# The last expert's w_down taken by column halves, with the next block's first slot and half of its first projection in between

## The chip, the cores and the metric

The kernel runs on one NeuronCore of a Trainium2 chip. The metric is the device time of one execution in microseconds (us). The engines are TensorE (PE; its weight loads are PEld), VectorE (DVE), ScalarE (ACT), GpSimd (POOL) and SyncE (SP), which issues nearly all transfers.

## The reference

Two blocks in float32 on 256 tokens of width 1024. The first is a mixing layer followed by a mixture of experts with expert choice; the second begins with a norm and the projections of two attentions.

```python
# first block, second half: 16 experts, each takes 32 tokens
xe = h2[idx]                                   # (16, 32, 1024)
a  = einsum('becd,edf->becf', xe, w_gate_e)    # 1024 x 2048 per expert
u  = einsum('becd,edf->becf', xe, w_up_e)
y  = einsum('becf,efd->becd', silu(a) * u, w_down_e)   # 2048 x 1024 per expert
x  = x + gate_f * scatter_add(y * vals, idx)
x  = rms_norm(x, g_final)
# second block
h  = rms_norm_2(x, mix_norm_g)
u  = h @ w_in                                  # q_diff = the first 512 of its columns
...
```

## The kernel before, in words

**Slots.** All weights pass through a ring of 16 places in SBUF, each 128 partitions x 2048 floats (1 MB, one *slot*). Slots are numbered through the whole kernel: the head, 16 experts of 24 slots (8 of gate, 8 of up, 8 of down), then the tail (`FIRST_TAIL` on). SP issues the loads in this order; each waits until the slot whose place it takes has been used. The count of used slots is the semaphore `slot_used`, which TensorE raises.

**One expert (`expert`, TensorE, line 1133 on).** The 32 tokens are the stationary operand, 128 rows by 32 columns, so four products can stand beside each other in four column groups of the array (`tile_position`), writing four partition groups of a PSUM bank. Gate and up: per slot four products, one in each group (line 1142). The hidden values are turned (line 1157) and kept as `act_t`. Down (line 1169): a slot holds 2 rows of the contraction per partition and all 1024 output columns; its four products go to 2 groups and 2 banks (bank 2 and bank 3, for the column halves n = 0 and 1). When all 8 slots are through, VectorE evicts bank 2 and bank 3 into `y` (line 2081), and TensorE scatters `y` back to token order with 128 x 256 products into banks 4 to 7, which hold the residual stream transposed: two products for each quarter q of the columns (line 1180). The last 8 down slots of the last expert are loaded one by one, each with 8 KB in one piece per partition.

**Second block's entry.** ScalarE and VectorE split the stream's quarters into a high and a low float32r part (`split_stream`: `ht_hi` on ScalarE, line 1385; `ht_lo` on VectorE, line 1773), and likewise each weight slot (`split_entry` for the halves of the first slot, lines 1400 and 1788; `split_ahead` for whole slots, lines 1380 and 1763). A projection of rows (`rows_product`) multiplies three combinations of the parts (lines 734 to 736): `q_diff` has 48 such products, in 4 pairs of k. Pair by pair it waits for the parts; after the third pair `turn_stream_back` (line 1207) turns the stream into rows again, which needs ScalarE's copies `xt` of all four quarters (`stream_kept`, line 1641). Then come `k_diff` and the rest of `TAIL_UNITS`. The two slots of `q_diff` are loaded after all down slots (lines 660 and 662); POOL loads the attention bias when the first of them has been used (line 716).

**The order around the change** is written out by hand, engine by engine; no planner is involved. `keep_busy(n)` (line 903) issues n products of constants into a bank whose content nobody needs; the kernel before uses it only at the start.

Of the kernel before, what the change touches and what calls it, by code (L numbers as in the profile page):

```python
# [24 lines left out]
P = 128  # L25
# [91 lines left out]
def build(nc, t, out):  # L117
    ctx = ExitStack()
    with ctx:
# [432 lines left out]
        def _(sp):  # L552
# [94 lines left out]
            for e, n in loads_between((NE - 2) * EXPERT_SLOTS, NE * EXPERT_SLOTS - 4):  # L647
                sp.wait_ge(slot_used, HEAD_SLOTS + released(e + n - 1))
                load_expert(NE // 2 - 1, e, n)
            for e in range(NE * EXPERT_SLOTS - 4, NE * EXPERT_SLOTS):  # L650
                sp.wait_ge(slot_used, HEAD_SLOTS + released(e))
                load_expert(NE // 2 - 1, e, 1)
            for n, src in enumerate(tail_stream):
                s = FIRST_TAIL + n

                sp.wait_ge(slot_used, FIRST_TAIL - TAIL_RING + n + 1 if n < TAIL_RING else s - TAIL_RING + 1)
                if s == first_slot["q_diff"]:
                    for half, name in enumerate(OPENING[0:2]):
                        rows = slice(2 * half, 2 * half + 2)
                        sp.dma_start(slot_in(s, k=FG, n=BANK)[:, rows, :], src[:, rows, :]).then_inc(opening_loaded[name], 16)  # L660
                else:
                    sp.dma_start(slot_in(s, k=src.shape[1], n=src.shape[2]), src).then_inc(loaded[place(s)], 16)
# [57 lines left out]
        def _(pe):  # L720
            mm = nc.tensor.matmul

            def end_first(ins):
                ins.then_inc(first_ready, 1)
# [13 lines left out]
            def split_slot(s, **dims):  # L738

                if s == first_slot["q_diff"]:  # L740
                    pe.wait_ge(first_lo, STEPS * len(OPENING) + 1)
                else:
                    pe.wait_ge(lo_ready, len([n for n in split_no if n <= s]))
                return [shaped(ring_r[p][:], **dims) for p in (part_place[s], place(s))]
# [88 lines left out]
            def rows_product(s, u, await_pair=None):  # L833

                for i in range(2):
                    w = split_slot(s + i, k=FG, n=BANK)
                    for pair in range(2) if await_pair else (None,):
                        if await_pair:
                            await_pair(2 * i + pair)
                        for tt in range(TT):  # L840
                            for kk in (2 * pair, 2 * pair + 1) if await_pair else range(FG):
                                k = FG * i + kk
                                last = split_product(bank(2 * (u % 2) + tt), [a[:, k, tt * P:(tt + 1) * P] for a in (ht_hi, ht_lo)],
                                                     [h[:, kk, :] for h in w], k == 0, k == KD - 1)
                            if k == KD - 1 and tt == 0:
                                end_first(last)
                        if await_pair and i and pair == 0:
                            turn_stream_back()
                    last.then_inc(slot_used, 1)

# [52 lines left out]
            def keep_busy(n):  # L903

                for _ in range(n):
                    mm(psum[:, 2, 0:P], ones, ones, start=True, stop=True)
# [218 lines left out]

            def expert(i, h, looped=False, side=False):
# [34 lines left out]
                pe.wait_ge(cur_ready, 2 * i + (h + 2))  # L1161

# [12 lines left out]
                for n in range(2):  # L1175
                    pe.wait_ge(y_ready, 4 * i + (2 * h + n + 1))
                    for q in (2 * n, 2 * n + 1):
                        for c in range(2):
                            at = (2 * q + c) * P - n * BANK
                            last = mm(bank(4 + q, c=2, s=SEQ)[:, c, :], y[:, n, at:at + P], gwt.rearrange("p t m -> p (t m)"),  # L1180
                                      start=False, stop=True, skip_group_check=True)
                        last.then_inc(scattered, 1)
# [10 lines left out]

            def await_entry(pair):

                pe.wait_ge(norm_lo, pair + 1)
                if pair == 1:
                    pe.wait_ge(lo_ready, split_no[first_slot["q_diff"]] + 1)
# [41 lines left out]
            for u, (name, slots) in enumerate(TAIL_UNITS):  # L1240
# [6 lines left out]
                elif name in ("z0", "z1"):  # L1247
                    transposed_product(first_slot[name], u, (ht_hi, ht_lo))
                elif name in IN2_CHUNK:
                    rows_product(first_slot[name], u, await_entry if u == 0 else None)  # L1250
# [83 lines left out]
        def _(act):  # L1334
# [58 lines left out]
            def split_entry(half):  # L1393

                s = first_slot["q_diff"]
                cols = slice(half * SLOT // 2, (half + 1) * SLOT // 2)
                act.wait_ge(opening_loaded[OPENING[half]], 16 * (STEPS + 1))
# [325 lines left out]
        def _(dve):  # L1723
# [45 lines left out]
            def split_pair(q, b, scale, at):  # L1769

                dve.wait_ge(norm_hi, at + q + 1)
                for k in (2 * q, 2 * q + 1):
                    ins = V.scalar_tensor_tensor(ht_lo[:, k, :], bank(b, c=2, s=SEQ)[:, k % 2, :], scale[:, k:k + 1],
                                                 ht_hi[:, k, :].bitcast(F32), ALU.mult, ALU.subtract)
                ins.then_inc(norm_lo, 1)

            def split_stream(q):
                split_pair(q, STREAM_BANKS[q], mix_gain, 0)

            def split_entry(half):  # L1780

                s = first_slot["q_diff"]
# [3 lines left out]
                else:  # L1786
                    dve.wait_ge(first_hi, STEPS * len(OPENING) + 1)
# [283 lines left out]
            def expert(i, h):  # L2071
# [6 lines left out]
                V.tensor_tensor(act_h, bank(1), sig_a, ALU.mult).then_inc(act_ready, 1)  # L2078
                dve.wait_ge(slot_used, 2 * EXPERT_SLOTS * i + (HEAD_SLOTS + (h + 1) * EXPERT_SLOTS))
# [9 lines left out]
            expert(NE // 2 - 1, 1)  # L2089
# [298 lines left out]
```

## Time and profile before

| | |
|---|---|
| runs of the kernel before | 1314.24 us median of 3 (1312.12 to 1315.41) |
| profiled execution | 1314.88 us, span 1313.1 us |
| mean granted TensorE clock | 0.875 of full |
| TensorE busy | 979.5 us (75%) |
| VectorE / ScalarE busy | 378.1 / 247.5 us |
| HBM read | 494.71 MB, 378 GB/s over the span |

All times in the rows count from the start of the span. The granted clock is TensorE's, as a share of 2.4 GHz: 0.50 is 1.2 GHz. A busy time of TensorE counts the modelled ends of pipelined products, so start-to-start distances tell more than the duration of one.

### The profile page before, as it was taken

What the parts mean: (1) busy time and instruction counts of PE and PEld (TensorE: products, weight loads), DVE (VectorE), ACT (ScalarE), POOL (GpSimd) and SP (SyncE); (2) the same over time, 40 slices, a digit from 0 to 9 for tenths busy, and PEclk for the clock granted to TensorE, in tenths of its full rate; (3) what the DMA queues carried; (4) which work ended last, traced back from release to release, by engine and by line L of the source; (5) the groups of instructions that cost most, each with busy time, mean ns of one, the idle gap of its engine ahead of it and who ended that gap; (6) DMA issues with size and microseconds to landing.
All of it is one profiled execution on the core that took longest, in us unless ns stands there. A gap on an engine that the chain in (4) does not pass through costs nothing.

```text
span 1313.1 us, 15613 instructions
## 1 busy us (share of the span) xinstructions
PE 979.5 (75%) x6766; PEld 559.6 (43%) x6766; DVE 378.1 (29%) x575; ACT 247.5 (19%) x375; POOL 21.6 (2%) x47
## 2 busy tenths in 40 slices
PE   8999999878665665655656655657556666899998
PEld 7999998323121221212121221212121221478988
DVE  4698866210000110000010100000010100388865
ACT  4453434001000000000000000000000000467744
POOL 2000200000000000000000000000000000000000
PEclk8999999988787888689798878888786887999999
DMA  9998999899999999999999999999999999965230
GB/s 336 389 377 311 321 389 414 351 430 430 427 434 428 431 431 431 426 434 433 431 431 431 426 431 437 431 430 431 429 427 436 429 430 421 392 234 161 97 128 33
DMA packets 70156, 496.43 MB, mean 378 GB/s; under 512 B 4794, under 2 KB 26954, under 8 KB 49632
## 3 DMA queue, kind: packets, MB, share of 16 engines
q1 hardware_dynamic: 67792, 489.11, 90.4%
q0 software_dynamic: 2080, 6.55, 1.5%
q8 instruction: 35, 0.57, 0.2%
q10 hardware_dynamic: 240, 0.11, 0.0%
q14 instruction: 9, 0.07, 0.0%
HBM read 494.71 MB, written 1.06 MB: 378 GB/s over the span
## 4 chain that ended last, share of the span: by engine, by line
DMA 56%; PE 42%; DVE 1%; issue 1%; ACT 0%; ACTq 0%; SPq 0%; DVEq 0%
DMA ring<-in_w_down_e 23%; DMA ring<-in_w_up_e 18%; DMA ring<-in_w_gate_e 15%; PE psum L734 8%; PE psum L735 8%; PE psum L736 8%; PE psum L1142 7%; PE psum L1169 4%; PE psum L1180 1%; PE psum L885 1%; PE psum L1222 1%; PE psum L1077 0%; DMA arena<-in_b_ada 0%; PE psum L797 0%; PE psum L1257 0%
## 5 line engine op out<-in xcount | busy, mean ns | idle before, releaser
L1142 PE MATMUL psum<-ring,arena 128*32 128x512 f32 x2048 | 304.2, 743 | 192.8 <-DMA ring<-in_w_up_e 111.6
L1169 PE MATMUL psum<-ring,arena 128*32 128x512 f32 x976 | 162.2, 800 | 98.1 <-DMA ring<-in_w_down_e 97.5
L1142 PEld LDWEIGHTS psum<-ring,arena 128*32 128x32 f32 x2048 | 70.8, 130 | 385.8 <-issue 179.0
L1169 PEld LDWEIGHTS psum<-ring,arena 128*32 128x32 f32 x976 | 42.8, 137 | 203.9 <-issue 143.7
L1763 DVE TENSOR_TENSOR ring_r<-ring,ring_r 128x2048 fp32r<-128x2048 f32 x49 | 111.1, 2289 | 36.6 <-ACT ring_r L1380 36.4
L1540 ACT ACTIVATE arena<-psum 128x512 f32<-128x512 f32 x16 | 9.6, 598 | 535.2 <-PE psum L1142 535.2
L734 PE MATMUL psum<-ht_hi,ring_r 128*128 128x256 f32 x384 | 109.5, 285 | 0.0
L735 PE MATMUL psum<-ht_lo,ring_r 128*128 128x256 f32 x384 | 108.1, 281 | 0.0
L736 PE MATMUL psum<-ht_hi,ring_r 128*128 128x256 f32 x384 | 107.6, 280 | 0.0
L2081 DVE TENSOR_TENSOR arena<-psum,arena 128x512 f32<-128x512 f32 x32 | 20.6, 686 | 290.0 <-PE psum L1169 290.0
L1380 ACT ACTIVATE ring_r<-ring 128x2048 fp32r<-128x2048 f32 x49 | 92.4, 1910 | 29.2 <-PE psum L736 24.1
L2074 DVE TENSOR_TENSOR arena<-psum,arena 128x512 f32<-128x512 f32 x16 | 11.1, 692 | 270.9 <-ACT arena L1540 270.9
L734 PE MATMUL psum<-ring_r,ht_hi 128*128 128x256 f32 (+1 forms) x256 | 87.0, 340 | 0.2 <-issue 0.2
L736 PE MATMUL psum<-ring_r,ht_lo 128*128 128x256 f32 (+1 forms) x256 | 86.9, 339 | 0.0
L735 PE MATMUL psum<-ring_r,ht_hi 128*128 128x256 f32 (+1 forms) x256 | 86.1, 336 | 0.0
L734 PEld LDWEIGHTS psum<-ht_hi,ring_r 128*128 128x128 f32 x384 | 72.1, 188 | 1.9 <-issue 1.5
L736 PEld LDWEIGHTS psum<-ht_hi,ring_r 128*128 128x128 f32 x384 | 72.5, 189 | 0.0
L735 PEld LDWEIGHTS psum<-ht_lo,ring_r 128*128 128x128 f32 x384 | 72.4, 189 | 0.2
L1180 PE MATMUL psum<-arena 128*128 128x256 f32 x256 | 61.4, 394 | 13.6 <-DVE arena L2081 13.6
L1544 ACT ACTIVATE arena<-psum 128x512 f32<-128x512 f32 x16 | 9.6, 597 | 297.5 <-PE psum L1157 297.5
L1180 PEld LDWEIGHTS psum<-arena 128*128 128x128 f32 x256 | 48.6, 195 | 36.4 <-DVE arena L2081 30.1
L734 PEld LDWEIGHTS psum<-ring_r,ht_hi 128*128 128x128 f32 x256 | 48.1, 188 | 6.4 <-issue 1.1
(291 smaller groups left out, 921.8 us busy)
## 6 DMA issues: line engine op xcount, KB each, us to landing
ring<-in_w_gate_e SPq DMA_DIRECT2D x23, 4096.0 KB, 33.4
ring<-in_w_up_e SPq DMA_DIRECT2D x22, 4096.0 KB, 33.0
ring<-in_w_down_e SPq DMA_DIRECT2D x21, 4096.0 KB, 33.8
ring<-in_w_up_e SPq DMA_DIRECT2D x16, 2048.0 KB, 36.5
ring<-in_w_in SPq DMA_DIRECT2D x31, 1024.0 KB, 9.7
ring<-in_w_gate_e SPq DMA_DIRECT2D x14, 2048.0 KB, 36.2
ring<-in_w_down_e SPq DMA_DIRECT2D x14, 2048.0 KB, 36.9
ring<-in_w_ada SPq DMA_DIRECT2D x16, 1024.0 KB, 10.3
```

The costliest lines, as they stand in the source:

```text
L734: mm(to, left[0], right[0], start=start, stop=False)
L735: mm(to, left[0], right[1], start=False, stop=False)
L736: return mm(to, left[1], right[0], start=False, stop=stop)
L885: last = mm(psum[32 * g:32 * g + 32, 6, st % 2 * P:(st % 2 + 1) * P], c_rep[:, k, :], w[:, kk, g * P:(g + 1) * P], start=(k == 0), stop=(k ...
L1142: last = mm(psum[32 * g:32 * g + 32, b, :].rearrange("s (q c) -> s q c", c=4), cur[h][:, k, :], w[:, g // 2, :, g % 2 * 4:g % 2 * 4 + 4], ...
L1169: last = mm(psum[32 * q:32 * q + 32, 2 + n, :], act_t[:, f % 4, (f // 4) * CAP:(f // 4 + 1) * CAP], w[:, kk, n * BANK:(n + 1) * BANK], sta ...
L1180: last = mm(bank(4 + q, c=2, s=SEQ)[:, c, :], y[:, n, at:at + P], gwt.rearrange("p t m -> p (t m)"), start=False, stop=True, skip_group_ch ...
L1222: last = mm(bank(4 + 2 * m + c, j=2, s=SEQ)[:, j, :], q[r, 2 * m + j, (a % 2) * P:(a % 2 + 1) * P], k[r, 2 * m + j, :], start=True, stop=T ...
L1380: f(ring_r[part_place[s]][:], ring[:, place(s), :], ACT.Copy).then_inc(hi_ready, 1)
L1763: V.tensor_tensor(ring_r[place(s)][:], ring[:, place(s), :], ring_r[part_place[s]][:].bitcast(F32), ALU.subtract).then_inc(lo_ready, 1)
L2074: V.tensor_tensor(sig_a, bank(0), sig_a, ALU.mult).then_inc(gated, 1)
L2081: V.tensor_tensor(y[:, n, :], bank(2 + n), gf_row[:, n * BANK:(n + 1) * BANK], ALU.mult).then_inc(y_ready, 1)
```

## The change

The eight last down slots of the last expert (called D0 to D7 here) are loaded by column halves: D0 to D3 hold all 2048 rows of the contraction for columns 0 to 511, D4 to D7 for columns 512 to 1023. In a slot each partition has 4 rows, each a piece of 2 KB, and its four products go to the four column groups of the array. The first slot of `q_diff` is loaded between D3 and D4, into the place of another slot that comes free sooner. `q_diff`'s second slot now comes in halves too.

TensorE's order at the end of the last expert was: 8 down slots, 4 quarters of scatter, `q_diff` pairs 0, 1, 2, turn of the stream, pair 3. It becomes: D0, 4 constants, D1, 4 constants, D2, 4 constants, D3, 2 constants; scatter of quarters 0 and 1; `q_diff` pair 0; D4, D5; pair 1; D6, D7; scatter of quarter 2 and 3; pair 2 (column by column of k), turn of the stream, pair 3. VectorE evicts the first half of `y` after D3 and the second half in two steps of 256 columns after D7. ScalarE and VectorE split the entry slots' halves and the quarters in the new order. The first entry slot counts as used together with D7, and the bias's load waits for that count.

```diff
@@ place
-            return TAIL_START + (s - FIRST_TAIL) % TAIL_RING
+            return tail_room[0] if s == FIRST_TAIL else TAIL_START + (s - FIRST_TAIL) % TAIL_RING
@@ sync
-            for e in range(NE * EXPERT_SLOTS - 4, NE * EXPERT_SLOTS):
-                sp.wait_ge(slot_used, HEAD_SLOTS + released(e))
-                load_expert(NE // 2 - 1, e, 1)
+            def load_last_down(j):
+                n, block, part = j // 4, j % 4 // 2, j % 2
+                rows = t["w_down_e"][0][NE - 1].rearrange("(b p k) n -> b p k n", b=2, k=KD)[block]
+                at = expert_place(last_down + j)
+                sp.wait_ge(slot_used, HEAD_SLOTS + released(last_down + j))
+                sp.dma_start(shaped(ring[:, at, :], k=4, n=BANK), rows[:, 4 * part:4 * part + 4, n * BANK:(n + 1) * BANK]).then_inc(loaded[at], 16)
+            def load_entry(i):
+                s = FIRST_TAIL + i
+                for half in range(2):
+                    rows = slice(2 * half, 2 * half + 2)
+                    done = loaded[place(s)] if i and half else opening_loaded[OPENING[2 * i + half]]
+                    sp.dma_start(slot_in(s, k=FG, n=BANK)[:, rows, :], tail_stream[i][:, rows, :]).then_inc(done, 16)
+            for j in range(4):
+                load_last_down(j)
+            sp.wait_ge(slot_used, FIRST_TAIL - RING + 1)
+            load_entry(0)
+            for j in range(4, 8):
+                load_last_down(j)
...
@@ tensor
+            def entry_pair(pair):
+                s = first_slot["q_diff"] + pair // 2
+                by_column = pair == 2
+                pe.wait_ge(*((part_lo, KD + 1) if by_column else (norm_lo, pair + 1)))
+                if pair % 2:
+                    pe.wait_ge(lo_ready, split_no[s] + 1)
+                else:
+                    pe.wait_ge(first_lo, STEPS * len(OPENING) + 1 + pair // 2)
...
+            def scatter(q):
+                for c in range(2):
+                    k = 2 * q + c
+                    last = mm(bank(4 + q, c=2, s=SEQ)[:, c, :], y[:, k // 4, k % 4 * P:(k % 4 + 1) * P], gwt.rearrange("p t m -> p (t m)"),
+                              start=False, stop=True, skip_group_check=True)
+                last.then_inc(scattered, 1)
+            def last_down(j):
+                n, at = j // 4, expert_place(NE * EXPERT_SLOTS - 8 + j)
+                arrived(pe, FIRST_TAIL - 8 + j)
+                w = shaped(ring[:, at, :], k=4, n=BANK)
+                for kk in range(4):
+                    f = 4 * (j % 4) + kk
+                    last = mm(psum[32 * kk:32 * kk + 32, 2 + n, :], act_t[:, kk, (f // 4) * CAP:(f // 4 + 1) * CAP], w[:, kk, :],
+                              start=(f < 4), stop=(f >= 12), tile_position=(0, 32 * kk))
+                return last
...
+            for j in range(4):
+                last_down(j).then_inc(slot_used, 1)
+                keep_busy(4 if j < 3 else 2, 3)
+            pe.wait_ge(y_ready, 2 * NE - 1)
+            scatter(0)
+            scatter(1)
+            entry_pair(0)
+            last_down(4).then_inc(slot_used, 1)
+            last_down(5).then_inc(slot_used, 1)
+            entry_pair(1)
+            last_down(6).then_inc(slot_used, 1)
+            last_down(7).then_inc(slot_used, 2)
+            for half in range(2):
+                pe.wait_ge(y_ready, 2 * NE + half)
+                scatter(2 + half)
...
+                elif name == "q_diff":
+                    entry_pair(2)
+                    turn_stream_back()
+                    entry_pair(3).then_inc(slot_used, 1)
@@ scalar
-            split_entry(0)
+            split_entry(0, 0)
             split_stream(0)
-            split_entry(1)
+            split_entry(0, 1)
             split_stream(1)
+            split_entry(1, 0)
             split_stream(2)
-            split("q_diff", 1)
             split_stream(3)
+            split_entry(1, 1)
@@ vector
-            split_entry(0)
+            dve.wait_ge(slot_used, FIRST_TAIL - 4)
+            V.tensor_tensor(y[:, 0, :], bank(2), gf_row[:, 0:BANK], ALU.mult).then_inc(y_ready, 1)
+            split_entry(0, 0)
             split_stream(0)
-            split_entry(1)
+            split_entry(0, 1)
             split_stream(1)
-            dve.wait_ge(scattered, 4 * NE)
+            dve.wait_ge(slot_used, FIRST_TAIL)
+            for half in range(2):
+                cols = slice(half * HALF, (half + 1) * HALF)
+                V.tensor_tensor(y[:, 1, cols], bank(3)[:, cols], gf_row[:, BANK + half * HALF:BANK + (half + 1) * HALF], ALU.mult).then_inc(y_ready, 1)
+            split_entry(1, 0)
             split_stream(2)
-            split("q_diff", 1)
             split_stream(3)
+            split_entry(1, 1)
```

## Rows read from the trace of the kernel before

**Rows 1.** The page's chain that ended last, by engine and by line.
```profile
DMA 56%; PE 42%; DVE 1%; issue 1%; ACT 0%; ACTq 0%; SPq 0%; DVEq 0%
...
DMA ring<-in_w_down_e 23%; DMA ring<-in_w_up_e 18%; DMA ring<-in_w_gate_e 15%; PE psum L734 8%; PE psum L735 8%; PE psum L736 8%; PE psum L1142 7%; PE psum L1169 4%; PE psum L1180 1%; PE psum L885 1%; PE psum L1222 1%; PE psum L1077 0%; DMA arena<-in_b_ada 0%; PE psum L797 0%; PE psum L1257 0%
```

**Rows 2.** Stretches of the span: length, busy time by engine, granted clock, DMA, GB/s.
```profile
1150.00:1313.10 163.10, 156.69 (x996) 137.68 (x994) 122.63 (x171) 101.38 (x172) 0.00 (x0) 1.00 0.39 129
1110.00:1116.50 6.50, 4.77 (x20) 1.32 (x20) 0.69 (x1) 0.23 (x1) 0.00 (x0) 0.50 1.01 422
1118.00:1120.00 2.00, 2.00 (x14) 0.40 (x6) 0.00 (x0) 0.37 (x2) 0.00 (x0) 0.50 0.98 410
1120.00:1122.50 2.50, 2.49 (x20) 0.51 (x14) 0.00 (x0) 0.00 (x0) 0.00 (x0) 0.99 1.01 423
1127.00:1137.00 10.00, 7.97 (x37) 4.03 (x34) 4.00 (x6) 3.57 (x7) 0.00 (x0) 1.00 1.04 387
1122.50:1130.60 8.10, 5.73 (x24) 1.13 (x24) 0.00 (x0) 0.00 (x0) 0.00 (x0) 1.00 1.02 405
```

**Rows 3.** TensorE in order of time: start, length, idle before and its releaser.
```profile
1100.85 3.64 PE L1142 MATMUL psum<-ring,arena 128*32 128x512 f32 x32 [2.31 <-DMA ring<-in_w_up_e]
...
1110.65 3.64 PE L1142 MATMUL psum<-ring,arena 128*32 128x512 f32 x16 [2.98 <-DMA ring<-in_w_up_e]
...
1116.92 5.57 PE L1169 MATMUL psum<-ring,arena 128*32 128x512 f32 x32 [0.69 <-ACT arena L1544]
```

**Rows 4.** The chain that ended last, in order of time, from 1099 us.
```profile
1099.05 31.52 DMA ring<-in_w_down_e
1130.61 1.94 PE psum L1169 x8
1132.57 0.70 DVE arena L2081
1133.32 3.72 PE psum L1180 x16
...
1145.35 1.75 PE psum L1207 x16
...
1149.87 0.23 PE psum L734
```

**Rows 5.** VectorE in order of time: a quarter's low parts, a slot's low part.
```profile
1135.36 0.88 DVE L1773 SCALAR_TENSOR_TENSOR ht_lo<-psum,arena,ht_hi 128x256 fp32r<-128x256 f32 x2 [0.37 <-ACT ht_hi L1385]
...
1145.12 2.29 DVE L1763 TENSOR_TENSOR ring_r<-ring,ring_r 128x2048 fp32r<-128x2048 f32 x1 [2.47 <-ACT ring_r L1380]
```

**Rows 6.** ScalarE: a quarter's high parts, half a slot, three stream copies, the fourth, a slot.
```profile
1134.49 0.84 ACT L1385 ACTIVATE ht_hi<-psum,arena 128x256 fp32r<-128x256 f32 x2 [1.47 <-PE psum L1180]
1135.21 1.05 ACT L1400 ACTIVATE ring_r<-ring 128x1024 fp32r<-128x1024 f32 x1
...
1140.11 1.62 ACT L1641 ACTIVATE arena<-psum 128x512 f32<-128x512 f32 x3
1142.68 0.60 ACT L1641 ACTIVATE arena<-psum 128x512 f32<-128x512 f32 x1 [0.96 <-DVE ht_lo L1773]
1143.17 1.91 ACT L1380 ACTIVATE ring_r<-ring 128x2048 fp32r<-128x2048 f32 x1
```

**Rows 7.** TensorE in the first stage: constants; wide products with narrow ones behind.
```profile
8.61 2.93 PE L906 MATMUL psum<-arena 128*128 128x128 f32 x12
...
24.55 0.28 PE L735 MATMUL psum<-ht_lo,ring_r 128*128 128x256 f32 x1
24.67 0.28 PE L736 MATMUL psum<-ht_hi,ring_r 128*128 128x256 f32 x1
24.88 1.96 PE L885 MATMUL psum<-ring,arena 128*32 128x128 f32 x64
```

**Rows 8.** POOL's issue of the bias, and its size and time to landing.
```profile
1142.88 0.70 POOL L716 DMA_DIRECT2D ring<-in_bias  x1 [881.81 <-PE psum L736]
...
ring<-in_bias POOLq DMA_DIRECT2D x1, 3072.0 KB, 13.6
```

More of the change, by code:

```diff
@@ L738, in split_slot @@
             def split_slot(s, **dims):
[L740 to L743, printed above, removed]
+                pe.wait_ge(lo_ready, len([n for n in split_no if n <= s]))
                 return [shaped(ring_r[p][:], **dims) for p in (part_place[s], place(s))]
@@ L831, in columns_rows, with rows_product @@
                 last.then_inc(slot_used, 1)
-            def rows_product(s, u, await_pair=None):
+            def rows_product(s, u):
                 for i in range(2):
                     w = split_slot(s + i, k=FG, n=BANK)
[L837 to L848, printed above, removed]
-                    last.then_inc(slot_used, 1)
+                    for tt in range(TT):
+                        for kk in range(FG):
+                            k = FG * i + kk
+                            last = split_product(bank(2 * (u % 2) + tt), [a[:, k, tt * P:(tt + 1) * P] for a in (ht_hi, ht_lo)],
+                                                 [h[:, kk, :] for h in w], k == 0, k == KD - 1)
+                        if k == KD - 1 and tt == 0:
+                            end_first(last)
+                    last.then_inc(slot_used, 1)
@@ new lines, in entry_pair @@
+            def entry_pair(pair):
[6 more added lines that the diff above has]
+                    pe.wait_ge(first_lo, STEPS * len(OPENING) + 1 + pair // 2)
+                w = [shaped(ring_r[p][:], k=FG, n=BANK) for p in (part_place[s], place(s))]
+                ks = (2 * pair, 2 * pair + 1)
+                for k, tt in [(k, tt) for k in ks for tt in range(TT)] if by_column else [(k, tt) for tt in range(TT) for k in ks]:
+                    if by_column and (k, tt) == (ks[1], 0):
+                        pe.wait_ge(norm_lo, pair + 1)
+                    last = split_product(bank(tt), [a[:, k, tt * P:(tt + 1) * P] for a in (ht_hi, ht_lo)],
+                                         [h[:, k % FG, :] for h in w], k == 0, k == KD - 1)
+                    if k == KD - 1 and tt == 0:
+                        end_first(last)
+                return last
@@ L1161, in expert @@
                 pe.wait_ge(cur_ready, 2 * i + (h + 2))
+                if not looped and i == NE // 2 - 1 and h == 1:
+                    return
                 for j in range(8):
@@ L1177, in expert @@
                     for q in (2 * n, 2 * n + 1):
[L1178 to L1182, printed above, removed]
+                        scatter(q)
                 if side:
@@ L1391, in split_stream, with split_entry @@
                 split_pair(q, STREAM_BANKS[q], mix_gain)
-            def split_entry(half):
-                s = first_slot["q_diff"]
+            def split_entry(i, half):
+                s = first_slot["q_diff"] + i
                 cols = slice(half * SLOT // 2, (half + 1) * SLOT // 2)
-                act.wait_ge(opening_loaded[OPENING[half]], 16 * (STEPS + 1))
+                if i and half:
+                    arrived(act, s)
+                else:
+                    act.wait_ge(opening_loaded[OPENING[2 * i + half]], 16 * (STEPS + 1))
                 if half == 0:
@@ L1774, in split_pair, with split_entry @@
                                                  ht_hi[:, k, :].bitcast(F32), ALU.mult, ALU.subtract)
+                    if by_column and k % 2 == 0:
+                        ins.then_inc(part_lo, 1)
                 ins.then_inc(norm_lo, 1)
             def split_stream(q):
-                split_pair(q, STREAM_BANKS[q], mix_gain, 0)
-            def split_entry(half):
-                s = first_slot["q_diff"]
+                split_pair(q, STREAM_BANKS[q], mix_gain, 0, by_column=q == 2)
+            def split_entry(i, half):
+                s = first_slot["q_diff"] + i
                 cols = slice(half * SLOT // 2, (half + 1) * SLOT // 2)
@@ L2068, in _, with expert @@
             take(1, 0)
-            def expert(i, h):
+            def expert(i, h, last=False):
                 dve.wait_ge(sig_ready, 2 * i + (h + 1))
@@ L2078, in expert @@
                 V.tensor_tensor(act_h, bank(1), sig_a, ALU.mult).then_inc(act_ready, 1)
+                if last:
+                    return
                 dve.wait_ge(slot_used, 2 * EXPERT_SLOTS * i + (HEAD_SLOTS + (h + 1) * EXPERT_SLOTS))
@@ L2088, in _ @@
             take(NE - 1, NE - 1)
-            expert(NE // 2 - 1, 1)
+            expert(NE // 2 - 1, 1, last=True)
             def split(name, i=0):
```

26 lines of the change are left out of this document (12 added, 14 removed).

## The prediction, made before the changed kernel had run

> **What bounds the kernel now.** I read the chain of work that ended last first [rows 1]: it consists of transfers (56%) and TensorE (42%), and the transfers are the three expert matrices. So the span has a part in which TensorE waits for weights and a part that is TensorE's own. The stage table [rows 2] shows where they meet: DMA moves 405 to 423 GB/s while TensorE is 71% busy between 1122.5 and 1130.6 us (5.73 of 8.10); from 1150 us to the end DMA moves 129 GB/s and TensorE is busy 156.69 of 163.10 us. The chain in order of time [rows 4] gives the seam: the last down slot is issued at 1099.05 and lands at 1130.6; its products take 1.94, the first eviction to `y` 0.70, the scatter 3.72, and then the second block's first projection, `q_diff`, runs. Three quarters of it (36 products from 1137.04 to 1145.35, 0.231 each), the turning back of the stream (1.75 from 1145.35) and its last quarter end where `k_diff` begins: 1149.87 us. After that nothing of the change is left on TensorE, so **the sum is the new time of this one event**.
>
> **The change, part by part.** I lay out the new order on TensorE from 1116.92 us, where the down products begin in both kernels [rows 3]; what comes before is the same.
>
> *Transfers.* A slot is 1.049 MB. Large contiguous pieces come at 423 GB/s, the strided 2 KB rows of `w_in` at 387 [rows 2], so 2.48 and 2.71 us each. The eight last down slots become 2 KB rows, and one entry slot goes ahead of the last four. The first of the eight starts to flow at about 1130.6 - 8 x 2.5 = 1110.6. New landings, one each 2.71: D0 to D3 at 1113.3, 1116.0, 1118.7, 1121.4; entry slot 0 at 1124.1; D4 to D7 at 1126.9, 1129.6, 1132.3, 1135.0. The last lands 4.4 later than now. SP gets one more wait ahead of D4 to D7 (first up slot used, about 1101.8, against 1099.05 for the last issue now [rows 3, 4]): behind it stand four loads with over 20 us to go until they are due, so it costs nothing. POOL's only queued load, the bias, waits for a count that now comes with D7, some 4 us sooner than 1142.88 [rows 8].
>
> *Down products.* Four products of one slot now go to four different column groups. Such slots took 3.64 / 4 = 0.91 us each at full clock and 3.64 / 2 = 1.82 at half (x32 is four slots, x16 two [rows 3]; their clock stands in [rows 2]); the present order takes 1.94 for a lone slot [rows 4].
>
> *Constant products.* Four of them are eight records of 128 columns. The turns of that width took 1.75 / 16 = 0.109 each at full clock [rows 4], so 0.87 for four; the opening's twelve records took 2.93, 0.24 each, 1.95 for four [rows 7]. I take 0.87 at full clock and twice that at half; the other end adds 0.1 to 1 us each.
>
> *Changes between the narrow and the wide array.* In the first stage wide products start 0.12 apart (24.55, 24.67) and the narrow one that follows starts 0.21 later (24.88) [rows 7]: 0.09 us per change. There are 11 where there was one: 1.0 us in all, 0.9 more than now. The lower end is zero, the upper 0.2 each; each is taken as 0.09 below. The Trainium skill's TensorEngine Tiling (Array Packing), section Key Properties, says that changing the tiling mode drains the array. The trace agrees in kind, with these 0.09 us.
>
> *The schedule.* The clock is 0.50 at 1116.92 and rises at 1120.0 [rows 2], under unbroken work, which there is again. D0 to 1118.74; constants, half of them slow, to 1120.29; D1 to 1121.29; constants 1122.25; D2 1123.25; constants 1124.21; D3 1125.21. All four slots landed by 1121.4, so the constants fill no gap here and stand on the path: 2.6 us of the first phase. `y`'s first half 0.70 (two constants hidden beside it), starts of 0.05 at both ends: scatter 0 and 1 run 1126.0 to 1127.86 (eight records at 3.72 / 16). ScalarE starts 0.24 behind scatter 0 as it does now (1133.32 + 0.93, 1134.49 [rows 4, 6]), 0.84 for the high part, VectorE 0.88 for the low [rows 5]: 1128.95, a wait of 1.1 for TensorE. The first pair is 12 products of 0.231: 1131.72. D4 and D5 1133.63, second pair 1136.49, D6 and D7 1138.40. **D7 landed at 1135.0 and TensorE gets to it at 1137.5: the transfers, 4.4 later, are hidden with 2.5 to spare**. Then the new serial tail: 256 columns of `y` 0.44 (by the 0.44 of one column of the low parts), scatter 2 to 1139.85, ScalarE 1140.1 to 1140.95, VectorE's single column to 1141.4, third pair to 1144.2. The stream may be turned back only when ScalarE has copied it: high part of quarter 3 to 1141.9, the last entry half 1.05, four copies of 1.62 / 3 [rows 6] to 1145.1. So TensorE waits 0.9 there, which now is covered (the copies end at 1143.3, the turn begins 1145.35). Turn to 1146.9, last pair to 1149.65.
>
> `k_diff` needs its first slot in both parts: ScalarE 1.91 from 1145.1, VectorE 2.29 [rows 5, 6]: 1149.4, just in time. Its slots land by 1140.5 and 1143.2, before the bias, which needs 13.6 from its issue [rows 8], takes much of the rate.
>
> *Sum.* 1149.65 against 1149.87: 0.2 us sooner. What is gained (24 projection products, 5.5; half the scatter, 1.9; narrower evictions and products, about 1.3) goes back into order: the old seam waited for the last slot at 1130.6; the new one starts its serial tail at 1138.4. The profiled execution took 1314.88, span 1313.1; so 1314.7 for such an execution, and against the median of the runs, 1314.24, **1314.0 us**.
>
> **Rivals.**
> *A, the engine keeps up.* If the clock is already high when D0 starts, 1.5 us go (0.9 of D0, 0.6 of the constants), and if the array changes cost nothing, 1.0 more: 1147.15 at the seam, 2.5 sooner than forecast, 1311.5. It cannot go much further, since TensorE then gets to D7 at 1135.0, where D7 lands. For it: the low stretch before 1120 follows two waits for up slots that need not fall alike. Against: those stages are not touched and the clock was 0.50 there. 22%.
>
> *B, slower by the clock.* TensorE was at half while it was busy 4.77 of 6.50 us from 1110 and 2.00 of 2.00 from 1118, and rose after the latter [rows 2]. If narrow products and constants of 128 columns do not bring it back as the old stream did, it stays low until D3 is through. The 5.2 us of work after 1120.0 then take 10.4, the seam comes at 1154.9, and the time is 1319. It decides from the rise at 1120.0 on: if the granted clock is still 0.50 at 1121, this is the case. The Trainium skill's TensorE: Matmul & The Clock Gate, section What's actually happening, has it that the throttled clock is the default and activity releases it; the trace agrees, and that activity is what the constants supply. 10%.
>
> *C, slower by the transfers.* If the 4 KB stride of half rows costs more than the rows of `w_in` do, the hidden 2.5 us are used up: nine slots at 300 GB/s, 3.5 each, bring D7 at 1142.1, 4.6 beyond TensorE's 1137.5, 1318.6. The rows at hand (387, also strided) leave it 6%. At 350 GB/s it costs nothing.
>
> *D, the bias comes too early.* It would start to flow around 1142 to 1143 and take the rate from `k_diff`'s second slot, for which ScalarE asks at 1149. That slot is due at 1143.2; only if it falls behind by 6 us does TensorE wait, by 1 us or so: 1315.0. 5%, and not told apart from the forecast by time.
>
> **How the numbers follow.** The forecast, seam within 1.5 us of now, has 57%: 1312.5 to 1315.5 by itself. With A, D, the runs' own spread of 1312.1 to 1315.4, and part of B and C, the range is 1310.5 to 1317.5. A change under 0.3% (3.9 us, about what such a measurement tells from none) holds the forecast, A and D, 84%; of these I give 10 to a gain beyond it, by waits that I charged and that are not there, and 2 to a loss. Of the 16% of B and C half cost more than 3.9 us (the clock may come back before D3, the rate lie between 300 and 350). So faster 0.10, same 0.80, slower 0.10.
>
> **What would show it.** Right: `q_diff`'s first products near 1129 and `k_diff`'s first near 1149.7; no wait of TensorE for a down slot after D3; a wait of about 1 us before the turn of the stream; the clock at 1.00 from 1120; D7's landing near 1135. Wrong: TensorE waiting for a down slot among the last four (transfers bind), a clock of 0.50 past 1121, the constants finishing ahead of landings (then they are free and the transfers are slower than I think), or a wait of `k_diff` for its slot.

## The result, and the profile after

The changed kernel takes 1318.22 us (median of 20 runs, 1314.81 to 1319.12) against 1314.28 for the kernel before (20 runs, 1312.12 to 1316.37): ratio 1.0027, interval 1.0021 to 1.0034, so 3.9 us slower, outside the range that was forecast. The same kernel measured a second time (changed_again, below) took 1316.92 against 1314.11, 2.8 slower. The profiled execution took 1318.11 us with a span of 1316.3.

TensorE in order of time in the changed kernel (start, length, line; in brackets the idle time before and its releaser). It answers to [rows 3] and [rows 4]. L1193 are the up products, L1173 the down products, L938 the constants, L1162 the scatter, L754 to L756 the projections, L1265 the turn of the stream.
```profile
1108.76 1.92 PE L1193 MATMUL psum<-ring,arena 128*32 128x512 f32 x16 [2.97 <-DMA ring<-in_w_up_e]
...
1112.93 1.07 PE L1173 MATMUL psum<-ring,arena 128*32 128x512 f32 x8 [0.69 <-ACT arena L1609]
1113.93 1.16 PE L938 MATMUL psum<-arena 128*128 128x128 f32 x8
...
1119.62 1.06 PE L1173 MATMUL psum<-ring,arena 128*32 128x512 f32 x8 [0.36 <-DMA ring<-in_w_down_e]
...
1121.49 1.99 PE L1162 MATMUL psum<-arena 128*128 128x256 f32 x8 [0.17 <-DVE arena L2309]
1127.44 1.92 PE L1173 MATMUL psum<-ring,arena 128*32 128x512 f32 x16
1132.26 1.92 PE L1173 MATMUL psum<-ring,arena 128*32 128x512 f32 x16
1134.74 1.99 PE L1162 MATMUL psum<-arena 128*128 128x256 f32 x8 [0.55 <-DVE arena L2317]
1140.64 1.94 PE L1265 MATMUL psum<-arena 128*128 128x128 f32 x16 [0.28 <-ACT arena L1707]
...
1145.19 0.39 PE L754 MATMUL psum<-ring_r,ht_hi 128*128 128x512 f32 x1
```
Everything up to the seam is there, and sooner than forecast: D0 starts at 1112.93, at full clock, the turn at 1140.64, and `k_diff`, the next projection, begins at 1145.19, 4.7 us before its old 1149.87 [rows 4]. Two of those microseconds are this execution's own: its last up products started at 1108.76, against 1110.65 [rows 3]. The start of those last up products (called U) lies ahead of everything that was changed on TensorE, so I compare executions from it on.

The loss comes after that. The chain that ended last, from 1129 us on (start, length, what):
```profile
1129.43 19.14 DMA ring<-in_w_in
1148.59 1.92 ACT ring_r L1442
1150.53 2.30 DVE ring_r L1829
1152.88 0.50 PE psum L754
...
1170.04 0.87 PE psum L1319 x8
1170.91 0.85 issue
1171.76 1.06 PE psum L1319 x8
1172.82 1.48 issue
1174.30 0.68 PE psum L1303 x4
1174.98 1.37 issue
1176.35 3.75 PE psum L1280 x15
```
Two things are new in it. A transfer of `w_in`, `k_diff`'s second slot, is 19.14 us under way and sets ScalarE, VectorE and TensorE in turn. And the attention's first scores (L1280, which were L1222) take 3.75, where the kernel before has 2.00:
```profile
1172.05 0.87 PE psum L1257 x8
1172.92 0.53 issue
1173.45 1.07 PE psum L1257 x8
1174.52 0.45 PE psum L1245 x4
1174.97 0.97 issue
1175.94 2.00 PE psum L1222 x16
```
Why the slot is late stands in the queues. The changed kernel, 1138.5 to 1148 us (q1 is SP's queue with the weights, q0 is POOL's, and in this window it holds only the bias; pieces, MB, share of the 16 engines):
```profile
q0 software_dynamic: 272, 3.15, 79.1%
q1 hardware_dynamic: 415, 0.82, 22.6%
```
The kernel before has the same pair of rows when its bias flows, 1146 to 1155.5 us, but by then both slots of `k_diff` have landed:
```profile
q0 software_dynamic: 268, 3.15, 78.1%
q1 hardware_dynamic: 439, 0.87, 23.8%
```
POOL's issue, which was at 1142.88 [rows 8], and those who wait for the slot, in the timelines:
```profile
1134.52 0.70 POOL L736 DMA_DIRECT2D ring<-in_bias  x1 [874.78 <-PE psum L1173]
...
1148.59 1.91 ACT L1442 ACTIVATE ring_r<-ring 128x2048 fp32r<-128x2048 f32 x1 [3.98 <-DMA ring<-in_w_in]
...
1150.53 2.29 DVE L1829 TENSOR_TENSOR ring_r<-ring,ring_r 128x2048 fp32r<-128x2048 f32 x1 [3.51 <-ACT ring_r L1442]
...
1152.88 0.50 PE L754 MATMUL psum<-ring_r,ht_hi 128*128 128x512 f32 x1 [1.98 <-DVE ring_r L1829]
```
And the stretches around the scores (as in [rows 2]):
```profile
1170.90:1176.30 5.40, 1.75 (x13) 1.38 (x12) 5.28 (x8) 4.20 (x7) 0.00 (x0) 0.92 0.63 194
1176.30:1182.50 6.20, 6.15 (x22) 4.76 (x23) 3.62 (x5) 0.00 (x0) 0.00 (x0) 0.52 0.01 3
```
TensorE is busy 1.75 of 5.40 us while VectorE is busy 5.28 of them; then its granted clock is 0.52 for six microseconds.

### The profile page after: what moved, and what is told of

Its sections match the earlier page's. It is cut to its first block, busy times and chain, and to the rows that moved or that the text cites. A ratio compares the mean times of both kernels' runs of the same rounds, so it can differ in the third digit from the quotient of the medians.

```text
span 1316.3 us, 15673 instructions
## 1 busy us (share of the span) xinstructions
PE 970.6 (74%) x6794; PEld 560.3 (43%) x6794; DVE 378.6 (29%) x577; ACT 247.5 (19%) x376; POOL 21.4 (2%) x47
## 3 DMA queue, kind: packets, MB, share of 16 engines
HBM read 494.71 MB, written 1.06 MB: 377 GB/s over the span
## 4 chain that ended last, share of the span: by engine, by line
DMA 56%; PE 39%; SPq 2%; DVE 2%; issue 1%; ACT 0%
DMA ring<-in_w_down_e 21%; DMA ring<-in_w_up_e 18%; DMA ring<-in_w_gate_e 15%; PE psum L754 7%; PE psum L755 7%; PE psum L756 7%; PE psum L1193 7%; PE psum L1222 4%; DMA ring<-in_w_in 2%; SPq L561 1%; SPq L571 1%; PE psum L1280 1%; PE psum L1162 1%; PE psum L1155 1%; PE psum L1319 0%
## 5 line engine op out<-in xcount | busy, mean ns | idle before, releaser
L1193 PE MATMUL psum<-ring,arena 128*32 128x512 f32 x2048 | 297.8, 729 | 196.0 <-DMA ring<-in_w_up_e 115.3
L1193 PEld LDWEIGHTS psum<-ring,arena 128*32 128x32 f32 x2048 | 69.8, 128 | 386.1 <-issue 173.4
L1222 PE MATMUL psum<-ring,arena 128*32 128x512 f32 x912 | 143.7, 781 | 99.9 <-DMA ring<-in_w_down_e 99.9
L1222 PEld LDWEIGHTS psum<-ring,arena 128*32 128x32 f32 x912 | 38.8, 134 | 190.4 <-issue 134.4
L754 PE MATMUL psum<-ht_hi,ring_r 128*128 128x256 f32 x384 | 109.4, 285 | 0.0
L756 PE MATMUL psum<-ht_hi,ring_r 128*128 128x256 f32 x384 | 107.5, 280 | 0.0
L754 PE MATMUL psum<-ring_r,ht_hi 128*128 128x256 f32 (+1 forms) x256 | 87.9, 343 | 3.8 <-DVE ring_r L1829 2.0
L756 PE MATMUL psum<-ring_r,ht_lo 128*128 128x256 f32 (+1 forms) x256 | 87.1, 340 | 0.0
L1162 PE MATMUL psum<-arena 128*128 128x256 f32 x256 | 63.9, 405 | 13.5 <-DVE arena L2151 12.7
L754 PEld LDWEIGHTS psum<-ht_hi,ring_r 128*128 128x128 f32 x384 | 72.2, 188 | 1.9 <-issue 1.5
L756 PEld LDWEIGHTS psum<-ht_hi,ring_r 128*128 128x128 f32 x384 | 72.5, 189 | 0.0
L1162 PEld LDWEIGHTS psum<-arena 128*128 128x128 f32 x256 | 50.1, 201 | 37.7 <-DVE arena L2151 29.0
L754 PEld LDWEIGHTS psum<-ring_r,ht_hi 128*128 128x128 f32 x256 | 48.4, 189 | 12.6 <-issue 2.6
## 6 DMA issues: line engine op xcount, KB each, us to landing
ring<-in_w_gate_e SPq DMA_DIRECT2D x14, 2048.0 KB, 36.4
```

Of the source, the lines that this page charges most:

```text
L754: mm(to, left[0], right[0], start=start, stop=False)
L756: return mm(to, left[1], right[0], start=False, stop=stop)
L1162: last = mm(bank(4 + q, c=2, s=SEQ)[:, c, :], y[:, k // 4, k % 4 * P:(k % 4 + 1) * P], gwt.rearrange("p t m -> p (t m)"), start=False, sto ...
L1193: last = mm(psum[32 * g:32 * g + 32, b, :].rearrange("s (q c) -> s q c", c=4), cur[h][:, k, :], w[:, g // 2, :, g % 2 * 4:g % 2 * 4 + 4], ...
L1222: last = mm(psum[32 * q:32 * q + 32, 2 + n, :], act_t[:, f % 4, (f // 4) * CAP:(f // 4 + 1) * CAP], w[:, kk, n * BANK:(n + 1) * BANK], sta ...
```

## The experiments

All of them compute the whole reference. Each was timed against the kernel before on the same chip; the theories are the early bias, the clock, VectorE's list, and the seam.

**The bias alone.** late_bias is the changed kernel with POOL's wait one count later:
```
-            pool.wait_ge(slot_used, first_slot["q_diff"] + 1)
+            pool.wait_ge(slot_used, first_slot["q_diff"] + 2)
```


> The changed kernel with one edit: POOL issues the bias when the second slot of q_diff is used, not the first (with D7). Theory (bias): the bias's 12 KB pieces took the rate from k_diff's second slot, which landed at 1148.6 instead of about 1141; TensorE then waited 2.0 us for it, the chain behind waited 2.2 more around 1171 to 1176, and the clock fell to half for 6.5 us, about 3 us. Without it all of that goes: some 5 to 7 us faster than the changed kernel, so 1311 to 1313, ratio to before about 0.998; k_diff's second slot lands by 1142 (counted with the ups as in the changed kernel), no clock at 0.50 after 1160. Rival (late issue): that slot is late because SP may only issue it when D5 is used, after pair 0 of q_diff; then it stays late, TensorE still waits about 2 us, and the time stays within 1 us of 1318.

Measured 1314.49 (11 runs, 1312.62 to 1318.48), ratio 1.0002 (0.9993 to 1.0011). So one count of one wait takes away the loss. In the same 9.5 us window SP's queue now moves 3.50 MB in place of 0.82:
```profile
q1 hardware_dynamic: 1760, 3.50, 102.8%
```
The slot itself is issued at 1133.43 here, 4.0 us later than in the changed kernel (1129.43), and ScalarE still takes it up without a wait: so it was not a late issue that made it late, which was the rival. The 1311 to 1313 that I expected did not come, though: the loss goes, the seam's gain does not show in the time.

**The reverse.** before_early_bias is the kernel before, its bias let go at D7:
```
-            pool.wait_ge(slot_used, first_slot["q_diff"] + 1)
+            pool.wait_ge(slot_used, FIRST_TAIL)
```


> The kernel before with one edit: POOL issues the bias when all down slots are used (about 1132.6 instead of 1142.9). The bias theory: it then flows from about 1136.5 to 1146 and holds up k_diff's second slot (due 1141) to about 1148, as in the changed kernel. There ScalarE asks for it at 1148.1 and TensorE at 1155.5, so the old order has the room: 0 to 1 us slower than before, 1314 to 1315.5. If instead it costs 3 us or more, the early bias is enough by itself, whatever the order.

Measured 1316.35 (1314.01 to 1318.48), ratio 1.0017 (1.0008 to 1.0026): 2.2 us slower than the 1314.13 beside it, where I had expected 0 to 1. I had thought that the old order left the slots a margin. Its timelines (of the slowest of its 11 runs, 1318.48) show `k_diff`'s first slot late by 1.89 and the scores slow again, at 0.62 of the clock from 1178 to 1182.5:
```profile
1133.00 0.70 POOL L716 DMA_DIRECT2D ring<-in_bias  x1 [869.74 <-PE psum L1169]
...
1145.34 1.92 ACT L1380 ACTIVATE ring_r<-ring 128x2048 fp32r<-128x2048 f32 x1 [1.89 <-DMA ring<-in_w_in]
...
1177.68 3.40 PE L1222 MATMUL psum<-ring 64*128 64x256 f32 x16 [1.36 <-issue]
```
The early bias thus costs 2.2 us in the old order. In the new one it is 3.7 (1318.22 against late_bias) or 2.4 (changed_again against it), so that it costs more there is not shown.

**The constants.** late_bias_no_constants has no constants between D0 and D3 either:
```
-                keep_busy(4 if j < 3 else 2, 3)
```


> As late_bias, and the 14 constant products between D0 and D3 left out. Theory 1 (constants on the path): in the changed kernel's trace D0, constants, D1, constants, D2 follow without a gap, and only D3 waited 0.4 us for its landing; without constants D3 is still bound by its landing, so nothing is gained, 0 to 0.3 us. Theory 2 (they hold the clock): without them TensorE is busy about 1.0 us in 2.7, the clock falls to 0.50 before the scatter, and the 9 us of products up to the second pair take up to twice as long: 2 to 5 us slower than late_bias. I expect theory 2, with 1314 to 1317.

Measured 1314.23 (1313.13 to 1315.46), ratio 1.0002 (0.9993 to 1.0011): the constants neither help nor cost by the median, and the 2 to 5 us that I expected to lose are not there. Without them TensorE waits at D2 and D3 (0.58 and 1.66) for landings, but its clock is low at the first scatter (3.35 for 1.99). That trade is read from one trace each. The same trace shows something that I did not look for: the scores are slow with no slot late, behind the same waits (0.53, 0.69, 1.36) that late_bias's trace has with the clock up (0.53, 0.68, 1.36):
```profile
1173.72 3.54 PE L1279 MATMUL psum<-ring 64*128 64x256 f32 x16 [1.36 <-issue]
```
The stretches before and behind the start of the scores, first in late_bias, then in late_bias_no_constants (PEclk is the third number from the end):
```profile
1171.00:1176.70 5.70, 3.15 (x23) 2.42 (x21) 5.56 (x8) 4.60 (x7) 0.00 (x0) 1.00 0.60 184
1176.70:1183.00 6.30, 6.27 (x35) 5.19 (x36) 5.02 (x7) 0.00 (x0) 0.00 (x0) 1.00 0.01 3
...
1168.00:1173.70 5.70, 3.15 (x23) 2.41 (x22) 5.55 (x8) 4.60 (x7) 0.00 (x0) 0.98 0.61 184
1173.70:1180.00 6.30, 6.28 (x28) 5.06 (x29) 3.98 (x5) 0.00 (x0) 0.00 (x0) 0.75 0.00 0
```

**The column halves alone.** halves_only keeps the new tiles, the early constants and the narrow scatter, but loads D0 to D7 in a row and runs all of `q_diff` behind them:
```
-            for j in range(4):
+            for j in range(8):
                 load_last_down(j)
...
-            entry_pair(0)
-            last_down(4).then_inc(slot_used, 1)
-            last_down(5).then_inc(slot_used, 1)
...
+            for j in range(4, 8):
+                last_down(j).then_inc(slot_used, 1)
+                if j < 7:
+                    keep_busy(4)
...
+            entry_pair(0)
+            entry_pair(1).then_inc(slot_used, 1)
```


> Column halves of w_down alone: D0 to D7 in sequence with constants between all of them, first half of y evicted and scattered after D3, the entry slot loaded behind D7 and q_diff's four pairs all after the last scatter; the bias is issued when q_diff's first slot is used, as before. Theory (sum by rows): the 2 KB pieces bring D7 1.9 us later (8 x 0.24), the tail behind D7 shrinks from 1.94 + 0.7 + 3.72 to 0.95 + 0.4 + 1.9, which is 3.1 less: 1.2 us faster than before, 1313. Rival: the transfers do not land later, since only the entry slot's place in the order counts: 3.1 faster, 1311.

Measured 1314.46 (1312.59 to 1318.47), ratio 1.0004 (0.9995 to 1.0013). The bias goes out at 1142.81 there, as before, and nothing is lost; nor is the 1 us gained that I had expected. In its trace the turn of the stream comes 34.5 behind U, exactly as in the kernel before.

**The clock at the scores.** changed_hold_clock puts constants where TensorE stands before the scores: 3 ahead of the unit `turn_q_diff`, 3 ahead of `scale_row`, 5 ahead of the scores.
```
+                if name in ("turn_q_diff", "scale_row"):
+                    keep_busy(3, 4)
...
+                if name == "scale_row":
+                    keep_busy(5, 4)
```


> The changed kernel with constant products put into TensorE's waits ahead of the first scores: 3 ahead of turn_q_diff, 3 ahead of scale_row, 5 ahead of the scores, all into bank 4, which is free there. In the changed kernel TensorE stood 3.7 us between 1170.9 and 1176.4 and then ran 6.5 us at half clock. Theory (two costs in series: the late start of the scores, and the clock that falls at that wait): the scores still begin about 25.8 us after VectorE takes up k_diff's second slot, but at 1.00 behind them: 2 to 3 us faster than the changed kernel, 1315 to 1316. Rival (the fall is not worth much, or has another cause): 1318.

In its trace the clock holds: the stretch before the scores is 5.32 of 5.50 us busy, the scores take 2.00, and from them to the end it is 137.1 us, as in the kernel before (137.2), where the changed kernel takes 139.95:
```profile
1173.00:1178.50 5.50, 5.32 (x44) 4.85 (x42) 5.40 (x8) 4.60 (x7) 0.00 (x0) 1.00 0.61 191
1178.50:1184.00 5.50, 5.43 (x31) 4.53 (x32) 4.18 (x5) 0.00 (x0) 0.00 (x0) 1.00 0.01 3
```
But the time was 1317.56 (9 runs, 1312.36 to 1318.25), ratio 1.0021 (1.0009 to 1.0032), where I had expected 1315 to 1316. In the profiled run (1317.55, so a typical one) D0 came at 1117.78 and at half clock, and no slot was late; its U lay 0.9 later than in the kernel before's trace, and its scores came 67.1 behind U, against 65.3. So this execution lost 1.8 us ahead of the scores by another way than the late slot, and a fall of the clock at the scores isn't needed for a time near 1318. Beside the changed kernel's trace it shows what the fall costs where it happens, 2.8 us; as the cure of the median it failed.

**The same kernel again.** changed_again is the changed kernel, unaltered, beside the next ones.

> The changed kernel as it is, for a second trace beside the runs of this chip: 1318 median. The traces so far differ in when and at which clock TensorE starts D0 (1112.9 at 1.00 in the first trace of the changed kernel, 1117.8 at 0.50 in changed_hold_clock), and in whether k_diff's second slot comes late. Theory: the new order runs without slack from D0 on, so the end of q_diff follows D0's start by 32.3 us at full clock and about 1.1 more at half, and it is the early starts that have the late slot. I expect one of the two patterns, the sum within 1 us of 1318 in both.

Measured 1316.92 (11 runs, 1313.93 to 1318.73), ratio 1.0017 (1.0008 to 1.0026). The slot is late again (ScalarE waits 3.94), the scores take 3.42.

**VectorE's list.** Two steps that nobody awaits before the scores, `scale_x` (1.41) and a sum of squares (1.27), stand in VectorE's list ahead of what the scores need. In three kernels they move behind it:
```
-            scale_x()
...
-            qk_sums(2)
...
+            qk_sums(2)
...
+            scale_x()
```


> The kernel before, with two pieces of VectorE's work moved behind what the first scores need: scale_x (1.41 us) behind score_rows(0), and the sums of q_dil (1.45) behind unit turn_q_diff. Theory (VectorE's list sets the scores): in all six traces so far the scores begin 25.8 to 25.9 us after VectorE starts the low part of k_diff's second slot; in before TensorE stood 1.5 us there. With 2.9 us less in the list TensorE no longer waits there: 1.0 to 1.5 us faster, 1312.8 to 1313.2. Rival (TensorE bound throughout, as I took it in the prediction): no change, 1314.2.

> late_bias with the same two moves. Theory: late_bias stood 2.6 us in front of the scores (0.5, 0.7, 1.4), which took what its earlier end of q_diff had won; with 2.9 us less in VectorE's list nearly all of it comes out: 2.0 to 2.6 us faster than late_bias, 1311.8 to 1312.5, and 1 us or more below before_vector_relief. Rival: the list is not what those waits hang on: 1314.5.

> The changed kernel, its early bias kept, with the same two moves. Theory: k_diff's second slot is as late as it was (TensorE waits 2.0 us for it), but the scores begin 2.9 sooner, TensorE's wait there shrinks to under 1 us and the clock holds: 5 to 6 us faster than the changed kernel, 1312 to 1313.5. Rival (the late slot does the damage by TensorE's own 2.0 us and the rate lost, not by VectorE's list): 1316 to 1317.

Each ratio is to the kernel before that ran beside it: 1314.28 for changed, 1314.13 for late_bias, 1313.79 for the three with the shorter list.

| kernel | us (11 runs) | ratio | scores behind the low part of `k_diff`'s second slot |
|---|---|---|---|
| before | 1314.28 (20 runs) | 1 | 1175.94 - 1150.09 = 25.85 |
| changed | 1318.22 (20 runs) | 1.0027 | 1176.35 - 1150.53 = 25.82 |
| late_bias | 1314.49 | 1.0002 | 1176.73 - 1150.93 = 25.80 |
| before_vector_relief | 1313.60 (1312.61 to 1314.33) | 0.9998 (0.9989 to 1.0007) | 1174.97 - 1149.65 = 25.32 |
| late_bias_vector_relief | 1312.47 (1310.55 to 1314.95) | 0.9993 (0.9984 to 1.0002) | 1172.68 - 1148.72 = 23.96 |
| changed_vector_relief | 1313.87 (1312.56 to 1315.15) | 1.0001 (0.9992 to 1.0010) | 1176.23 - 1153.05 = 23.18 |

Of the 1.0 to 1.5 us that I expected in the old order 0.2 came, of the 2.0 to 2.6 in late_bias 2.0 (1.2 by the ratios), and the third kernel missed its 1312 to 1313.5 by 0.4.

The first three orders differ and the distance is the same within 0.05 us; over all nine traces with the old list it is 25.79 to 25.86. So VectorE's list sets it. With 2.7 us taken out of it the distance shrinks by 0.5 in the old order and by 1.8 to 2.6 in the new one. In the old order VectorE then waits for TensorE instead, 1.33 and 0.85 us at its two evictions ahead of the scores, so TensorE's own work sets the rest there. The changed kernel gets back 3.1 us (against changed_again) to 4.4 (against 1318.22), or 2.1 to 3.4 by the ratios, although its slot is as late as ever (ScalarE waits 3.86): the wait before the scores falls from 1.37 to 0.18, and the clock stays up:
```profile
1151.11 1.91 ACT L1442 ACTIVATE ring_r<-ring 128x2048 fp32r<-128x2048 f32 x1 [3.86 <-DMA ring<-in_w_in]
...
1176.23 2.00 PE L1280 MATMUL psum<-ring 64*128 64x256 f32 x16 [0.18 <-issue]
```

**The clock at D0.** late_bias_clock_before_D0 has late_bias's wait, and constants in the waits for the last up slots:
```
+                        if b and k in (4, 6) and not looped and i == NE // 2 - 1 and h == 1:
+                            pe.wait_ge(gwt_ready, 2 * i + (h + 1))
+                            keep_busy(k + 2, 3)
```


> late_bias with constants also in TensorE's waits for the last up slots of the last expert (6 after the fourth, 8 after the sixth), into bank 3, free by then. Theory: the clock is then at 1.00 when D0 starts, D0 comes at 1113 to 1115 and never at 1117, and q_diff ends 1 to 3 us sooner on average; but VectorE's list still sets the scores, which follow 25.8 us behind k_diff's second slot, so all of the shift that reaches VectorE's start counts: 1 to 2 us faster than late_bias, 1312.5 to 1313.5, with a narrower spread. Rival (the clock at D0 does not matter, the transfers bind): 1314.5.

Measured 1314.24 (1312.02 to 1315.15), ratio 1.0000 (0.9991 to 1.0009). D0 runs in 1.06 in its trace, where late_bias's trace has
```profile
1114.71 1.93 PE L1173 MATMUL psum<-ring,arena 128*32 128x512 f32 x8 [0.69 <-ACT arena L1609]
1116.58 2.08 PE L938 MATMUL psum<-arena 128*128 128x128 f32 x8
...
1144.64 1.94 PE L1265 MATMUL psum<-arena 128*128 128x128 f32 x16 [0.29 <-ACT arena L1707]
...
1176.73 2.00 PE L1280 MATMUL psum<-ring 64*128 64x256 f32 x16 [1.36 <-issue]
```
From D0 to the turn it is 29.93 there, 27.71 in the changed kernel's trace and 27.28 here: the clock at D0 is worth 2.2 to 2.6 us to the seam. The 1 to 2 us that I expected in the median are not there.

**All of it.** all_four joins the later bias, VectorE's list, and both sets of constants.

> The version that the traces point to: the changed kernel with the bias late, VectorE's two pieces moved, constants in the waits ahead of the scores and in those for the last up slots. The parts as they add by the theory: late_bias_vector_relief 1312.5, 1 us for the clock at D0, 0.3 for the scores: 1311 to 1311.8, ratio to before 0.998. Rival (the parts give the same microseconds twice): 1312.5.

Measured 1312.71 (11 runs, 1311.15 to 1314.93), ratio 0.9991 (0.9982 to 1.0000): 1.4 us under the 1314.11 of the kernel before, at the edge of what can be told, and above the 1311 to 1311.8 that I expected. Its trace (1311.17, one of its two fastest runs) has D0 at 1112.94, the scores at 1172.22 without a wait, and a span of 1309.4, against 1316.3 for the changed kernel whose D0 lay at 1112.93. late_bias_vector_relief, with 1312.47, is no worse with two of the four edits.

## Why the prediction was wrong

The sum stood on one sentence: "After that nothing of the change is left on TensorE, so the sum is the new time of this one event." **That is the step that failed.** The event came as forecast or sooner; but the change also let the bias go 8 us earlier, which made a later slot late, and between the seam and the end there is a place where VectorE sets the pace and not TensorE, so the gain ended there.

*The seam: right, with another rival's numbers.* I had D0 at 1116.92 with half the clock, and `k_diff` 32.7 us behind it. The changed kernel's trace had D0 at full clock and `k_diff` 32.3 behind it; late_bias's trace had the half clock and runs like the forecast (D0 1.93, constants 2.08, forecast 1.82 and 1.6), with the turn 29.9 behind D0 where I had 28.2. So a low clock at D0 costs 2.2 us to the turn, where I charged 1.5. The transfers kept 386 GB/s and TensorE waited for no slot among D4 to D7, as forecast; ahead of the turn it waited 0.28, not 0.9. Rival A thus held at the seam in that trace, 2.8 us sooner relative to U (36.4 behind it against 39.2), and its 1311.5 did not come.

The forecast also missed how much hangs on that clock. In the old order the turn came 34.5 us behind U in three traces (34.54, 34.46, 34.55), although the down products began 6.3, 4.2 and 5.8 behind it, by the clock: TensorE waits there for landings anyway. In the new one it came 31.5 to 31.9 behind U in five of the six traces with D0 at full clock (32.8 in the sixth), and 35.3 and 35.0 in the two with constants and D0 at half (late_bias, changed_hold_clock). So in these traces the new order is ahead by 1.7 to 3.1 us with the clock up at D0, and behind by 0.4 to 0.8 without.

*The bias: the rival was there, mis-sized.* D had the mechanism, and priced it at 1 us with 5%. Two of its terms were wrong. I had the bias flow from 1142 or 1143: it was issued at 1134.52 and flowed from about 1138.5. And I put no number on the rate that it would take; it got 79%, so the slot that was due at 1143.2 came at 1148.57. I had TensorE wait only with the slot "behind by 6 us": 5.4 behind, with the seam 4.5 early, would be a wait of 3.9 by that, and it was 1.98.

*The end of it: VectorE, then the clock.* The 1.98 is not the loss. At the scores it is 2.3 us, relative to U: 67.6 (1176.35 - 1108.76) against 65.3. With the seam 2.8 sooner than before, by the same measure, the scores still came later. They come 25.8 behind VectorE's start on the slot in all three orders above; I had read [rows 2], TensorE 156.69 of 163.10 us busy, as TensorE setting the pace throughout. That average hides the few microseconds in which it doesn't: already before, it stood 0.53 and 0.97 ahead of the scores, 1.5 in all. In late_bias, with no slot late, it stood 2.6; with the late slot 0.85, 1.48 and 1.37, 3.7 in all. Then the clock fell, and the next six microseconds ran at 0.52: 2.8 more to the end (139.95 against 137.2). 2.3 and 2.8, less 1.9 for this execution's earlier U, are the 3.2 between the two spans.

How far the fall of the clock explains the median is not shown. It came in both traces of the changed kernel and in before_early_bias's (2.8 us of standing), but of three traces with the same 2.6 us of standing it came in one (late_bias_no_constants) and not in the two others, and changed_hold_clock, without it, was no faster by the median.

What holds it together: with the bias later (1314.49) or VectorE's list shorter (1313.87) the loss is gone, each by itself; with the bias earlier in the old order (1316.35) 2.2 us of it appear.

*Two points on the clock.* The forecast has it rise at 1120.0; in the changed kernel's trace it was high from D0, and low where I had not looked, at 1176. In late_bias's it rose near 1120, between D1 (1.94) and the constants behind it (1.16). And rival B, a low clock through D3, didn't come in either.

*What stays open.* Why the runs of one kernel spread. Part of it lies ahead of the change: U itself lay between 1108.76 and 1111.51 in the traces. The 20 runs of the changed kernel lie in two bunches, five at 1314.8 to 1316.4 and fifteen at 1317.3 to 1319.1, which the 11 of changed_again (1313.9 to 1318.7) don't show. A fall of the clock at the scores would fit, but changed_hold_clock has a bunch near 1318 too, and its one trace shows no such fall. And whether the new order, with its faults mended, is faster by a microsecond or not at all.

## What to carry to other kernels

Where a step is moved, look up every wait by count that it satisfies on other engines: here a bias load on another queue came 8 us sooner and took four fifths of the rate from a slot with a due time. Follow a gain at a seam to the next place where TensorE stands, however short, and ask whose list ends that wait; if it is another engine's, the gain stops there. Where an order works without waits for landings, look at the clock at its start: the old order hid a low clock in its waits, the new one does not. And a stall of a few microseconds can cost twice, once as a wait and once as the clock behind it; in these traces it did so in some executions and not in others.

## What the runs showed of the hardware

- Two queues with work did not share evenly: the bias in large pieces (3.15 MB in 272) took 79.1% and the 2 KB pieces of `w_in` (0.82 MB in 415) 22.6%; 78.1 and 23.8 in the kernel before. The Trainium skill's DMA: Bandwidth & Descriptors, section Queues, rings and completion order, has each engine take turns between queues by packets. The rows agree in kind, if the pieces that the profile counts are those packets: their counts are far nearer to each other (272 to 415) than the bytes (3.15 to 0.82 MB).
- The strided 2 KB pieces of the halves and of `w_in` ran at 386 GB/s (1118 to 1134 us), where large contiguous ones made 405 to 423 [rows 2]. No run tells the size of the piece from the stride.
- TensorE, busy 1.75 of 5.40 us, ran the 6.2 us after it at 0.52, so nearly all of them at the lower of its two levels (1.2 GHz). The same waits can end either way: busy 3.15 of 5.70 us ahead of the scores, late_bias ran the next 6.3 us at 1.00 and late_bias_no_constants at 0.75.
